# Queries and keys of a hybrid decoder layer: projected with features on partitions, and the third block's residual added by GpSimd

## The reference, cut to what matters

```python
proj = jnp.einsum('bsd,de->bse', h, w_in)
q_a, k_a, v_a, q_i, k_i, w_i, q_r, k_r, v_r, g_r = jnp.split(proj, offsets, axis=-1)
q_a = _rope(q_a.reshape(B, S, ATT_HEADS, ATT_HEAD_DIM), positions)      # 8 heads x 64
k_a = _rope(k_a...), q_i = _rope(q_i...)                                # 8 heads x 64
k_i = _rope(k_i[:, :, None, :], positions)[:, :, 0, :]                  # one key of 64
q_r = _rope(q_r...), k_r = _rope(k_r...)                                # 4 heads x 128
# _rope: x1, x2 = the two halves of a head
#        [x1 * cos - x2 * sin, x2 * cos + x1 * sin]
```

```python
h_res = h_res + gate2 * _rms_norm(ffn, g_post_ffn)
```

## Time and profile before

| | |
|---|---|
| median of 3 runs | 699.95 us (696.12 to 700.84) |
| the profiled execution's own time | 699.4 us |
| its span in the trace | 697.6 us |
| PE busy | 640.6 us, 92% of the span, 2464 matmul records |
| DVE / ACT / POOL busy | 368.7 / 177.2 / 79.3 us |
| mean granted clock of TensorE | 0.972 of full speed |

### The profile page before, as it was taken

The page is one execution under the profiler, slowest core; times in us unless marked ns, Lnnn a source line. Parts: engine busy times, 40 slices in busy tenths (PEclk is TensorE's granted clock), DMA queues, the critical chain, the costliest instruction groups (busy, mean ns, idle before and its releaser), DMA issues.

```text
span 697.6 us, 7155 instructions
## 1 busy us (share of the span) xinstructions
PE 640.6 (92%) x2464; PEld 303.7 (44%) x2464; DVE 368.7 (53%) x733; ACT 177.2 (25%) x360; POOL 79.3 (11%) x96
## 2 busy tenths in 40 slices
PE   1599999999999999999979999989999999998883
PEld 1364444444344444455644457433434453333331
DVE  4864366998776764416883335872232423242055
ACT  1430111134233443541121223112221212121023
POOL 1012121210011111000000000111211121110101
PEclk9999999999999999999989997999999999998997
DMA  9994706060704225070098219799999999999996
GB/s 319 394 384 150 245 7 235 2 239 1 241 1 149 94 62 181 1 249 31 25 385 343 91 60 351 277 366 394 419 419 420 420 419 418 420 417 413 409 410 143
DMA packets 53139, 174.45 MB, mean 250 GB/s; under 512 B 10224, under 2 KB 10224, under 8 KB 42224
## 3 DMA queue, kind: packets, MB, share of 16 engines
q1 hardware_dynamic: 45136, 160.29, 59.6%
q0 software_dynamic: 6160, 12.10, 5.4%
q10 hardware_dynamic: 1808, 1.61, 0.7%
HBM read 168.20 MB, written 15.21 MB: 263 GB/s over the span
## 4 chain that ended last, share of the span: by engine, by line
PE 82%; DVE 6%; DMA 5%; issue 3%; ACT 2%; SPq 1%; DVEq 0%; ACTq 0%; POOLq 0%
PE psum L763 31%; PE psum L1053 14%; PE psum L1114 8%; PE psum L919 7%; DMA both_bufs<-pair_rows 3%; DVE work L1447 2%; PE psum L1026 2%; PE psum L876 2%; PE psum L896 2%; PE psum L884 2%; PE psum L841 2%; PE psum L833 1%; PE psum L850 1%; PE psum L783 1%; PE psum L904 1%
## 5 line engine op out<-in xcount | busy, mean ns | idle before, releaser
L763 PE MATMUL psum<-ring,hT 128*128 128x512 f32 x496 | 221.2, 599 | 0.0
L763 PEld LDWEIGHTS psum<-ring,hT 128*128 128x128 f32 x496 | 92.6, 191 | 115.9 <-issue 115.5
L1053 PE MATMUL psum<-ring,hT 128*64 128x512 f32 (+2 forms) x320 | 92.2, 594 | 2.2 <-DMA ring<-in_w_up_exp 1.8
L1879 DVE TENSOR_SCALAR work<-work 128x256 f32<-128x256 f32 x16 | 4.7, 291 | 101.6 <-PE psum L1063 75.8
L1053 PEld LDWEIGHTS psum<-ring,hT 128*64 128x64 f32 (+2 forms) x320 | 31.7, 142 | 49.2 <-issue 46.3
L1447 DVE SCALAR_TENSOR_TENSOR rows<-ring,sm,rows 128x512 f32<-128x512 f32 x64 | 51.0, 797 | 1.7
L1335 ACT ACTIVATE work<-psum 128x256 f32<-128x256 f32 x17 | 6.5, 384 | 146.8 <-PE psum L1053 146.8
L1114 PE MATMUL psum<-ring,work 128*64 128x512 f32 (+1 forms) x160 | 40.1, 598 | 0.7 <-ACT work L1341 0.7
L2015 POOL TENSOR_TENSOR both_bufs<-both_bufs 128x256 f32<-128x256 f32 (+1 forms) x21 | 17.0, 809 | 175.7 <-DVE both_bufs L1505 145.1
L1053 PE MATMUL psum<-both_bufs,hT 128*64 128x512 f32 x64 | 31.0, 641 | 3.3 <-issue 3.3
L2062 POOL DMA_INDIRECT pair_rows<-work,pid_t x16 | 16.0, 1000 | 153.2 <-DVE work L1891 153.2
(11 more groups left out here) (310 smaller groups left out, 881.7 us busy)
## 6 DMA issues: line engine op xcount, KB each, us to landing
ring<-in_w_down_exp SPq DMA_DIRECT2D x20, 1024.0 KB, 18.2
ring<-in_w_in SPq DMA_DIRECT2D x8, 2048.0 KB, 9.4
ring<-in_w_ada SPq DMA_DIRECT2D x8, 2048.0 KB, 14.0
ring<-in_w_gate_exp SPq DMA_DIRECT2D x14, 1024.0 KB, 19.9
ring<-in_w_up_exp SPq DMA_DIRECT2D x14, 1024.0 KB, 22.8
ring<-in_w_ada SPq DMA_DIRECT2D x7, 1024.0 KB, 13.7
ring<-in_w_gate_exp SPq DMA_DIRECT2D x12, 512.0 KB, 15.2
ring<-in_w_up_exp SPq DMA_DIRECT2D x12, 512.0 KB, 15.7
```

Of the source, the lines that this page charges most:

```text
L763: mm = pe.matmul(o[:, 0:width], hT3[:, k, b * P:(b + 1) * P], w[:, k, :], start=(k == 0), stop=(k == KD - 1))
L1053: mm = pe.matmul(o[rows, :], XT[u % 2][:, k, rows], both(GU_SLOT[place])[:, k, :, :], start=(k == 0), stop=(k == KD - 1))
```

## The change

Queries and keys (`TURNED`: qi, kw, ka, qa, qr, kr) are now all projected the way kw was: a unit is 128 feature columns by the tokens, so `w` is the weight and hT moves. qi has four units of 384 tokens in place of three of 512. No `turn` is left on PE, and no copy of it on ACT. Instead DVE multiplies by the cosine straight into qiT, kaT and so on, and by a signed sine into `CROSS`; ACT issues DMAs that exchange the halves of the heads between partitions (four of 32 partitions for heads of 64, two of 64 for heads of 128), from `CROSS` to `SWAPPED`; POOL adds `SWAPPED` to the destination in one operation. The tables become 2 x (cosine, sine) of 128x512, one pair for each head size, made by 18 operations on DVE and 4 on ACT. `idx` waits for all of kw and qi to be rotated, `att` for all of qa, the first retention score for all of kr. The positions come as a broadcast row; `decay` is loaded at the chunk of gr, behind the last rotation. At the end, SP loads the residuals of blocks 2 and 3, POOL adds that of block 2 in halves, and SP stores four halves.

```diff
@@ PE @@
-                for k in range(KD):
-                    mm = pe.matmul(o[:, 0:width], hT3[:, k, b * P:(b + 1) * P], w[:, k, :], ...)
+                    if name == "kw":
+                        mm = pe.matmul(o[0:KW, :], w[:, k, :], hT3[:, k, :], ...)
+                    elif name in TURNED:
+                        mm = pe.matmul(o[:, at], w[:, k, b * P:(b + 1) * P], hT3[:, k, at], ...)
+                    else:
+                        mm = pe.matmul(o[:, :], hT3[:, k, b * P:(b + 1) * P], w[:, k, :], ...)
-            def turn(name, b):
-                pe.wait_ge(roped, r + 1)
-                for c in range(4):
-                    mm = pe.transpose(o[:, c * P:(c + 1) * P], src[:, c * P:(c + 1) * P], ident)
...
-                pe.wait_ge(*brought(("turn", "kw", 0)))
-                pe.wait_ge(*brought(("turn", "qi", b)))
+                pe.wait_ge(*rotated("kw"))
...
-                pe.wait_ge(*brought(("turn", "qa", b)))
+                pe.wait_ge(*rotated("qa"))
@@ ACT @@
-            a.activation(sinT[:, :], sinT[:, :], ACT.Sin).then_inc(trig_ready, 1)
-            a.activation(cosT[:, :], cosT[:, :], ACT.Sin).then_inc(trig_ready, 1)
+            for n in range(2):
+                act.wait_ge(ang_ready, n + 1)
+                a.activation(trig[:, n, 1, :], trig[:, n, 1, :], ACT.Sin, bias=zero, scale=sign of n)
+                a.activation(trig[:, n, 0, :], trig[:, n, 0, :], ACT.Sin).then_inc(trig_ready, 1)
+            def swap(s):
+                act.wait_ge(rope_ab, r + 1)
+                if r >= 2:
+                    act.wait_ge(roped, r - 1)
+                for n, here in enumerate(rows):
+                    there = rows[(n ^ 1) % 2] if kind == "kw" else rows[n ^ 1]
+                    act.dma_start(SWAPPED[r % 2][here, at], CROSS[r % 2][there, at]).then_inc(...)
@@ DVE @@
             def angles():
+                link(v.tensor_copy(posf, posi))
+                for n in range(2):
+                    (9 operations of 128x512 in a chain: 5 tensor_scalar, 4 scalar_tensor_tensor)
             def rotate(s):
+                dve.wait_ge(trig_ready, 2 * table + 2)
+                if r >= 2:
+                    dve.wait_ge(roped, r - 1)
+                v.tensor_tensor(dst[rows, at], o, trig[rows, table, 0, at], ALU.mult)
+                v.tensor_tensor(CROSS[r % 2][rows, at], o, trig[rows, table, 1, at], ALU.mult)
@@ POOL @@
-                for dst in rooms:
-                    g.tensor_tensor(dst[:, :, 0, :], xc[:, :, 0, :], xs_[:, :, 1, :], ALU.subtract)
-                    ins = g.tensor_tensor(dst[:, :, 1, :], xc[:, :, 1, :], xs_[:, :, 0, :], ALU.add)
+                pool.wait_ge(swapped[r % 2], swaps_to(r))
+                g.tensor_tensor(dst, dst, SWAPPED[r % 2][:, at], ALU.add).then_inc(roped, 1)
...
-            for b in range(NB - 1):
+            for b in range(NB - 2):
                 pool.dma_start(out_blocks[b], YG[b][:, 1, :], accum_op=ALU.add).then_inc(y_both[b], 16)
+            pool.wait_ge(y_scaled, NB - 1)
+            for c in HALVES:
+                y = YG[NB - 2][:, 1, c]
+                g.tensor_tensor(y, y, x3[:, NB - 2, c], ALU.add).then_inc(o_sum, 1)
@@ SP @@
-            for part, c in enumerate(HALVES):
-                sp.wait_ge(o_add, part + 1)
-                sp.dma_start(out_blocks[NB - 1][:, c], YG[NB - 1][:, 1, c]).then_inc(o_out, 16)
+            for b, part in ((NB - 2, 0), (NB - 1, 0), (NB - 1, 1), (NB - 2, 1)):
+                sp.wait_ge(o_sum if b == NB - 2 else o_add, part + 1)
+                sp.dma_start(out_blocks[b][:, HALVES[part]], YG[b][:, 1, HALVES[part]]).then_inc(o_out, 16)
```

More of the change, by code:

```diff
@@ L130, in shape_constants @@
     c[:, C_ONES:C_ONES + P] = 1.0
-    c[:, C_FREQ:C_FREQ + 64] = np.float32(10000.0) ** (-np.arange(64, dtype=np.float32) / np.float32(64))
+    for n, half in enumerate((DH // 2, RDH // 2)):
+        c[:, C_TRIG + 2 * n] = np.float32(10000.0) ** (-(i % half).astype(np.float32) / np.float32(half))
+        c[:, C_TRIG + 2 * n + 1] = np.where(i // half % 2 == 0, 1.0, -1.0)
     c[:, C_IOTA:C_IOTA + P + 1] = np.arange(P + 1)
@@ L181, in __init__ @@
         self.steps = []
-        waiting = None
         use(("modA",), 6)
@@ L190, in __init__ @@
             name = ("unit", s, b)
-            if waiting == ("turn", "kw", 0):
+            if (s, b) == ("ka", 0):
                 use(("kwback",), 7)
@@ L312, in build @@
         kiT = work[:, 8192:8704]
-        kwT = retbuf[0:KW, 1024:1024 + S]
+        head_wts = retbuf[DH:KW, 0:S]
+        into = {"qi": qiT, "ka": kaT, "qa": qaT}
+        trig = xs[:, 2048:4096].rearrange("p (n f t) -> p n f t", n=2, f=2)
+        posi = ropebuf[:, 0:S].bitcast(I32)
+        posf, turns = xs[:, 0:S], xs[:, S:2 * S]
+        CROSS = [ropebuf[:, i * S:(i + 1) * S] for i in range(2)]
+        SWAPPED = [ropebuf[:, (2 + i) * S:(3 + i) * S] for i in range(2)]
         decay = xs[:, 2048:4096].rearrange("p (h t) -> p h t", h=RHEADS)
@@ L496, in used_up, with rotated, pieces, swaps_to @@
             return wout_done, NB
+        def rotated(kind):
+            return roped, plan.rope[("unit", kind, last_block(kind))] + 1
+        def pieces(kind):
+            half = (RDH if kind in ("qr", "kr") else DH) // 2
+            return [slice(at, at + half) for at in range(0, P, half)]
+        def swaps_to(r):
+            return sum(16 * len(pieces(u[1])) for u, n in plan.rope.items() if n <= r and n % 2 == r % 2)
+        def tokens(kind):
+            return slice(P if kind == "qi" else 0, S)
         def brought(use):
@@ L1231, in _ @@
             act.dma_start(rb[:, NG:NG + NE], prow(t["b_expert"], NE)).then_inc(post_in, 16)
-            into = {"qi": qiT, "qr": qrT, "kr": krT, "ka": kaT, "qa": qaT}
+            def swap(s):
+                kind = s[1]
+                r, at = plan.rope[s], tokens(kind)
+                act.wait_ge(rope_ab, r + 1)
+                if r >= 2:
+                    act.wait_ge(roped, r - 1)
+                rows = pieces(kind)
+                for n, here in enumerate(rows):
+                    there = rows[(n ^ 1) % 2] if kind == "kw" else rows[n ^ 1]
+                    act.dma_start(SWAPPED[r % 2][here, at], CROSS[r % 2][there, at]).then_inc(swapped[r % 2], 16)
             for s in steps:
@@ L1240, in _ @@
                     act.wait_ge(unit_done, plan.unit[s] + 1)
-                    a.activation(kwT, bank(s)[0:KW, :], ACT.Copy).then_inc(kw_out, 1)
+                    a.activation(head_wts, bank(s)[DH:KW, :], ACT.Copy).then_inc(kw_out, 1)
                 elif s[0] == "unit" and s[1] == "gr":
@@ L1244, in _ @@
                     a.activation(gr[:, s[2], :], bank(s)[:, :], ACT.Exp, scale=-1.0).then_inc(g_exp, 1)
-                elif s[0] == "turn":
-                    name, b = s[1:]
-                    if name == "kw":
-                        bring(s, kiT)
-                    else:
-                        bring(s, into[name][:, :, b * P:(b + 1) * P])
+                elif s[0] == "sums" and s[1] in TURNED:
+                    swap(("unit",) + s[1:])
                 elif s[0] == "idx":
@@ new lines, in rotate @@
+                r, at = plan.rope[s], tokens(kind)
+                table = 1 if kind in ("qr", "kr") else 0
+                rows = slice(0, DH if kind == "kw" else P)
+                dst = kiT if kind == "kw" else into[kind][:, g, :]
+                dve.wait_ge(unit_done, plan.unit[s] + 1)
+                dve.wait_ge(trig_ready, 2 * table + 2)
+                if r >= 2:
+                    dve.wait_ge(roped, r - 1)
+                if kind == "kw":
+                    dve.wait_ge(kw_out, 1)
@@ new lines, in rotate @@
+                if (kind, g) == ("ka", 0):
+                    dve.wait_ge(kw_turned, 1)
+                    back = bank(("kwback",))[:, 0:NB * HEADS].rearrange("p (b h) -> p b h", b=NB)
+                    link(v.tensor_scalar(wi, back, IDX_SCALE, None, ALU.mult))
+                o = bank(s)[rows, at]
+                v.tensor_tensor(dst[rows, at], o, trig[rows, table, 0, at], ALU.mult)
+                if kind == "kw":
+                    v.tensor_tensor(dst[DH:2 * DH, :], o, trig[rows, table, 0, :], ALU.mult)
@@ L1521, in mask_of @@
+                v.tensor_tensor(CROSS[r % 2][rows, at], o, trig[rows, table, 1, at], ALU.mult).then_inc(rope_ab, 1)
             def mask_of(b):
@@ L1786, in _ @@
                     kind, b = s[1:]
[L1787 to L1789 removed]
+                    if kind != "kw" and b < NB - 1:
+                        ada(ADA_BESIDE[kind], b, NB - 1)
                 elif s[0] == "keys":
@@ L2021, in bias @@
                 pool.dma_start(accB[0:1, :], b_ada[m:m + 1, :]).then_inc(bias_in, 16)
-            turns = [("turn",) + s[1:] for s in plan.rope]
             g.memset(accB, 0.0).then_inc(accB_clear, 1)
```

187 lines of the change are left out of this document (63 added, 124 removed).

## The result

The changed kernel takes 710.62 us in the median of five executions (706.98 to 713.77), the kernel before in the same set 699.58 (696.12 to 700.84): 1.0174 times before, 95% interval 1.0138 to 1.0210. A second set on the same code gave 1.0141 (1.0113 to 1.0169). It is slower, by 10 to 12 us. The execution that left the trace is the fastest of the five, 706.98 us with a span of 705.1; before it was 699.4, close to its median, with a span of 697.6. So the two traces differ by 7.5 us only, less than the medians.

A forecast was written before the change was run, and what follows sets the result against it. The prediction took PE, 82% of the chain that ended last, as the bound. Turns -8.8, tables +4.1, kw +2.1, qa +2.7, clock +5.1 and end -1.8 summed to +3.4 on 699.4: 703 us, range 693 to 712.

The forecast's parts named there:

- rival B: Exchanges queue behind loads, landing in 7.5 us; kw and qa waits cost +5.5 and +6.2; 715 us; chance 0.15.
- The landing ... I take 4: kw and qa exchanges: 4 us from issue to landing beside loads, PE gaps of 2.8 and 3.4 us.
- DVE is busy without a gap: From qa 0 on, DVE works without a gap, so PE's gain doesn't bring qa 3's products forward.
- E + 29.3: Time DVE ends qa 3's products, 142.0 us, counted from the end of qa 0 on PE, 112.70.
- The broadcast positions ...: nothing, within 0.7 us: Start: 256 KB of positions replace 512 small pieces and cost nothing, within 0.7 us either way.
- The tables, 4.1: Before the third qi unit: DVE's table work of 12.1 us leaves PE a new gap, +4.1 us.
- The clock, 5.1: Behind the three new gaps: PE's granted clock falls, 1.7 us for each, +5.1 us.
- the prediction's own example: PE idle for 2.28 us, then a granted clock of 0.66 over 360 to 370 us, 3.4 us of lost work.
- The turns, -8.8: On PE: 20 units lose their turn, 0.44 us each, -8.8 us.
- The end, -1.8: Last additions and stores: the end moves from 696.4 to 694.6, -1.8 us.
- Rival D: At the end DVE and POOL lock each other out, so the end stays where it was; 704.6 us; chance 0.05.
- Rival A: The gaps stay small: exchanges land in about 2 us and the clock holds; 693.3 us; chance 0.18.
- rival C: DVE is the bound from qa 0 to kr 3, so twelve turns give nothing; 707 us; chance 0.05.

The follow-up runs named there:

- E4: Changed kernel with SP holding the loads that take kw's and qa's slots until POOL has added the exchanged halves: 0.9998 times the kernel before.
- E9: Changed kernel with only the load that takes kw's slot held until kw's exchange is added: 1.0040 times the kernel before.
- E10: Changed kernel with only the load that takes qa's slot held until the last qa unit is added: 1.0072 times the kernel before.
- E1: Changed kernel with the b_ada bias rows asked for by ACT's queue instead of POOL's: 1.0075 times the kernel before.
- E11: Kernel before with the 256 KB broadcast positions load added, into a buffer nobody reads then: 1.0063 times the kernel before.
- E6: Changed kernel with PE doing unused products (2, 6 and 8) ahead of the three waits: 1.0083 times the kernel before.
- E0: Changed kernel run again without any edit: 1.0141 times the kernel before.
- E3: Changed kernel with the broadcast positions asked for after x has landed: 1.0089 times the kernel before.
- E5: Kernel before with only the change's new end (POOL's additions, four stores): 0.9979 times the kernel before.
- E2: Changed kernel with the second pair of tables (for qr and kr) made after kw's rotation: 1.0104 times the kernel before.
- E7: Changed kernel with E1 to E4 together and loads held for qi, kw, ka, qa and kr: 0.9937 times the kernel before.
- E8: E7 with qi's slots held until kw is added and positions asked for after the inverse root: 0.9847 times the kernel before, 687.6 us.

## Why the prediction was off

It said 703 us and most likely no change; it is 710.6 and slower. The time lies inside the range of 693 to 712 us, near its upper end; it is the width of the range that takes it in, and not the sum. The forecast had the right gaps, at the right places and from the right causes. What came lies between it and rival B (715 us), which was to decide from a landing of about 5 us on. The sum of +3.4 came out 6 to 9 us low, at these steps:

- **"The landing ... I take 4."** This is the step that failed. It is 6.0 to 6.1 us at both exchanges that count, and 2.0 when no load is beside them (E4 at both, E9 at kw, E10 at qa). The prediction had both numbers, 1.8 and 7.5, and took a middle one because the exchange is small. That didn't help: 64 KB issued 2 to 3 us (kw) and 5 to 7 us (qa 3) behind 4 MB took nearly as long as the 512 KB. The four issues also took 2.5 us and not 1.8. The gap at kw is 5.47 in place of 2.8, that at qa 7.34 in place of 3.4, the latter only in part by the landing. Rival B had 5.5 and 6.2 us for the two waits; they cost 4.7 and 6.7. It was given 0.15.
- **"DVE is busy without a gap".** It was; it is so no longer. POOL's queue holds the bias row behind the addition for ka 3, a step moved behind a new wait. The prediction looked at what stands behind ACT's new waits and not at what stands behind POOL's. Qa 3's products ended at E + 30.5 in place of E + 29.3, and E1 gains 5 to 7 us. The sum had no term for this.
- **"The broadcast positions ...: nothing, within 0.7 us."** +2.5 us here, 1.6 to 2.4 in the seven other traces of the same start. The start is bound by loads, as the step itself said, and 256 KB ahead of x delay it (E11).
- **The tables, 4.1.** The mechanism is right, 2.31 us in size. The 18 operations and the cast took 10.8 us and not 12.1: tensor_scalar between SBUF buffers 0.43, and scalar_tensor_tensor 0.69 in place of 0.75.
- **The clock, 5.1.** In this trace it is 1.8 + 2.3 + 2.0 = 6.1 us in the units behind the three gaps, and 0.5 more in the first index score (1.31 us in place of 0.79). E6 shows that it is a cost by itself. But it is no fixed price. At the third qi unit two units took 12.25 to 12.28 us behind gaps of 2.06 to 2.52 us (changed kernel, E1, E4, E9, E10) and 10.59 behind 1.95 and 1.51 (E0, E3). At the first attention score a gap of 3.27 us (E4) was followed by a loss of 2.9, one of 8.46 (E3) by 1.5. And the prediction's own example, the wait of 2.28 us at 360.86 with a unit of 9.21 us behind it, comes with 2.31 us at 373.43 in the changed kernel; the granted clock falls there too (0.66 from 373 to 378 us), but is back before the unit at 377.58, which takes 7.13.
- **The turns, -8.8.** 0.43 each, -8.6. **The end, -1.8.** -1.6 in the traces, and -1.5 alone in E5. Rival D's mechanism is seen in part: POOL's two additions take 3.94 us and DVE's two halves 2.79 in place of 1.42, but the end came sooner all the same.

With the sizes measured in this pair of traces the sum is: start +2.5, turns -8.6, tables +2.3, kw +4.7, qa +6.7 (the bias row in it), clock +6.6, end -1.6, together +12.6.

The two traces differ by 7.5, because they also differ in stretches that the change doesn't touch. The one of before had two slow spells that the other lacks: at MOD and the unit behind it at 180 us 10.7 us for 9.0, and 9.21 for 7.13 at 364.83, 3.8 us in all. Without the end that leaves 10.4, and at 402.22 us (412.91 in the changed kernel) the trace is 10.7 late. Then the routing: from 32 small matmuls at 419.72 (430.41) to the next step at 434.85 (441.72) it took 15.1 us before, at a granted clock down to 0.50, and 11.3 in the changed kernel, at full clock; waits behind it gave 1.5 us of that back. It is 8.4 late after that, and 9.1 at DVE's first sum of the end.

The sum's +12.6 lies near the 10 to 12 us of the two sets of timings, but each trace is one execution, and the start and the clock behind the gaps differ between executions by a microsecond or two; so that closeness is in part luck. The slow unit at the output projection came in seven of the experiments too (8.9 to 9.4 us: E2, E4 to E7, E9, E10), and not in E0, E1, E3, E8 and E11; the routing took 15.0 to 15.2 us in eight, 12.7 in E0, E3 and E8, 11.3 in E1. What decides it stays open.

Rival A fell with the gaps, and rival C too: in qr and kr PE has no new gap, and the eight turns there gave 3.2 us.

## What to carry to other kernels

Moving data between partitions by DMA in place of TensorE trades 0.43 us of a busy engine for a latency, and that latency is set by what is in the DMA engines: in these runs 2 us alone, 6 beside bulk loads. Where such a small transfer is waited for soon, hold back the load that starts in the same microseconds until it has landed, if the load has time; a hold in the wrong place only moves the load beside the next one. And when an instruction in a queue gets a new wait, read what stands behind it in that queue, and who waits for that.

## What the runs showed of the hardware

- 256 KB read from one row for 128 partitions delay a start bound by loads by 3.7 us, where 256 KB are 0.7 us at the 394 GB/s that the page of before shows for its second slice (17.4 to 34.9 us). In E11 SP's first six issues took 12.0 us, where they took 8.9 before. Why the broadcast is that dear wasn't tried.
- DVE and POOL, both with two inputs in SBUF, slow each other at the end. POOL's halves took 2.27 and 1.70 us, and an addition of that size with DVE on PSUM 1.26; DVE's took 1.11 and 1.75, and 0.71 without POOL. Each loses about 1.4 us, which fits taking turns as well as a slowdown of both. DVE's addition at 696.81 (L1960), beside POOL's first half, kept its 1.22 us, so there POOL alone was slowed:

```profile
696.88 3.94 POOL L2093 TENSOR_TENSOR both_bufs<-both_bufs,xs 128x512 f32<-128x512 f32 x2 [0.24 <-ACT both_bufs L1407]
```

```profile
698.58 2.79 DVE L1984 SCALAR_TENSOR_TENSOR both_bufs<-both_bufs,sm,xs 128x512 f32<-128x512 f32 x2
```

- PE's clock, once fallen, doesn't come back at once with work: the filling products of E6 at 155 us, after 3.45 us idle, took 8.83 us where eight take 6.9 at the full clock. The granted clock was 0.66 from 155 to 160 us and 1.00 from 160 to 164.
